# One comparison instead of four: the seat selection of an expert pair in a two-layer MoE kernel

## What is computed

```python
def hierarchical_moe(u, w_router_group, w_router_expert, w_gate, w_up, w_down):
    ...
    combine = (g_onehot[:, :, None] * (p_g[:, :, None] * w_in_group[:, None, :])).astype(x.dtype)
    y = jnp.zeros_like(x)
    for g in range(N_GROUPS):
        hid = jax.nn.silu(jnp.einsum('nd,edf->nef', x, w_gate[g])) * jnp.einsum('nd,edf->nef', x, w_up[g])
        y = y + jnp.einsum('nef,efd->nd', hid * combine[:, g, :, None], w_down[g])
```

## Time and profile before

| what | value |
|---|---|
| runs of the kernel before, median | 2497.47 us |
| profiled execution, its own time | 2503.42 us |
| profiled execution, span of the trace | 2501.6 us |
| TensorE matmul busy | 2353.1 us, 94% of the span |
| VectorE busy | 1884.0 us, 75% |
| ScalarE busy | 1359.9 us, 54% |
| HBM traffic | 241 GB/s over the span |

### The profile page before, as it was taken

How to read it: one execution, slowest core, us unless ns; L and a number is a source line. 1 busy time by engine, 2 the same in 40 slices (tenths; PEclk the granted TensorE clock), 3 DMA queues, 4 the chain that set the end, 5 groups by cost and what they waited for, 6 DMA issues and landing times.

```text
span 2501.6 us, 29914 instructions
## 1 busy us (share of the span) xinstructions
PE 2353.1 (94%) x11078; PEld 1732.6 (69%) x11078; DVE 1884.0 (75%) x2285; ACT 1359.9 (54%) x1497; POOL 20.5 (1%) x39
## 2 busy tenths in 40 slices
PE   7998999999997987999999998999989999988998
PEld 6556877777775465777777776456578865844987
DVE  2746999999997454999999998877467856564665
ACT  3235988898885142888888986126423312102332
POOL 0000000000000000000000000100000000000000
PEclk9998999999998988999999999999999999998999
DMA  9313988988886311788899888652156742532460
GB/s 330 114 68 146 375 355 365 379 358 354 354 366 255 134 68 67 322 362 357 357 370 380 359 358 334 208 184 103 68 195 242 278 151 101 200 136 76 165 240 18
DMA packets 115417, 603.67 MB, mean 241 GB/s; under 512 B 5208, under 2 KB 8352, under 8 KB 90556
## 3 DMA queue, kind: packets, MB, share of 16 engines
q1 hardware_dynamic: 111536, 588.83, 60.6%
q0 software_dynamic: 3792, 13.62, 1.6%
HBM read 601.38 MB, written 1.05 MB: 241 GB/s over the span
## 4 chain that ended last, share of the span: by engine, by line
PE 54%; DVE 20%; issue 13%; ACT 9%; DMA 2%; DVEq 1%; SPq 0%; ACTq 0%
PE bank L950 11%; DVE slab_parts L2640 8%; ACT high L1865 6%; PE bank L1260 4%; PE bank L1582 3%; PE bank L1212 3%; PE bank L1076 3%; PE bank L1239 3%; PE bank L1201 2%; PE bank L1511 2%; PE bank L1513 2%; PE bank L1512 2%; PE bank L1492 2%; PE bank L1494 2%; PE bank L994 2%
## 5 line engine op out<-in xcount | busy, mean ns | idle before, releaser
L2640 DVE TENSOR_TENSOR slab_parts<-ring,high 128x2048 fp32r<-128x2048 f32 x384 | 862.1, 2287 | 39.2 <-ACT high L1865 34.7
L1865 ACT ACTIVATE high<-ring 128x2048 fp32r<-128x2048 f32 x384 | 728.5, 1914 | 43.3 <-PE bank L1212 35.6
L1709 ACT ACTIVATE arena<-bank 128x512 f32<-128x512 f32 (+4 forms) x174 | 95.6, 587 | 401.5 <-PE bank L1582 90.3
L1212 PE MATMUL bank<-high,xT_parts 128*128 128x512 f32 x1024 | 294.3, 409 | 18.0 <-DVE slab_parts L2640 14.1
L1212 PE MATMUL bank<-slab_parts,xT_parts 128*128 128x512 f32 x1024 | 279.2, 394 | 0.0
L950 PE MATMUL bank<-ring,xT 128*128 128x512 f32 (+3 forms) x576 | 239.8, 578 | 9.1 <-ACT xT L1709 4.1
L1212 PEld LDWEIGHTS bank<-high,xT_parts 128*128 128x128 f32 x1024 | 184.5, 190 | 78.6 <-DVE slab_parts L2640 38.5
L1212 PEld LDWEIGHTS bank<-slab_parts,xT_parts 128*128 128x128 f32 x1024 | 194.0, 189 | 45.6
L1871 ACT ACTIVATE arena<-bank 64x512 f32<-64x512 f32 (+2 forms) x352 | 184.8, 534 | 62.4 <-PE bank L1239 52.1
L950 PEld LDWEIGHTS bank<-ring,xT 128*128 128x128 f32 x576 | 111.1, 194 | 135.4 <-issue 124.7
L2307 DVE TENSOR_TENSOR slab_parts<-ring,high 128x2048 fp32r<-128x2048 f32 x64 | 145.7, 2290 | 60.1 <-ACT high L1729 59.6
(11 more groups left out here) (373 smaller groups left out, 3536.1 us busy)
## 6 DMA issues: line engine op xcount, KB each, us to landing
ring<-in_moe_w_gate SPq DMA_DIRECT2D x64, 2048.0 KB, 8.6
ring<-in_moe_w_up SPq DMA_DIRECT2D x64, 2048.0 KB, 9.2
ring<-in_moe_w_down SPq DMA_DIRECT2D x64, 2048.0 KB, 9.0
ring<-in_mlp_w SPq DMA_DIRECT2D x32, 2048.0 KB, 12.8
ring<-in_w_mod SPq DMA_DIRECT2D x24, 2048.0 KB, 8.8
ring<-in_even_w_in SPq DMA_DIRECT2D x7, 2048.0 KB, 21.6
ring<-in_odd_w_in SPq DMA_DIRECT2D x6, 2048.0 KB, 10.5
ring<-in_h_w_in SPq DMA_DIRECT2D x6, 2048.0 KB, 8.1
```

Of the source, the lines that this page charges most:

```text
L1212: last = mm(dst[:, :], seated2[:, 4 * half + k, e], part_[:, k, :], start=(half == a == k == 0), stop=(half == a == 1 and k == 3))
L1865: act_fn(hi, weight_half(layer, name, half), ACT.Copy).then_inc(sem(f"high{layer}"), 1)
L2640: v.tensor_tensor(low, w, hi.bitcast(F32), ALU.subtract).then_inc(sem(f"low{layer}"), 1)
```

## The change

Each call of `take_seats` made four comparisons, one for each expert and tile, of the 64 seat numbers with one value per token (a scalar operand read per partition). It now makes one, of a tensor with a tensor: the seat numbers repeated over tiles and experts against the ranks repeated over the seats, 2 x 2 x 64 = 256 elements per partition. What is written to `sel` and the count on the semaphore stay the same.

```diff
             def moe_short(layer):
                 def take_seats(i):
 
-                    for e in range(2):
-                        for t in range(NT):
-                            last = v.tensor_scalar(sel[:, t, e], seats, rank[:, t, bass.ds(i * 2 + e, 1)], None,
-                                                   ALU.is_equal)
-                    last.then_inc(sem(f"seats{layer}"), 1)
+                    of_pair = [P, NT, 2, SEATS]
+                    v.tensor_tensor(sel, seats.unsqueeze(1).unsqueeze(1).to_broadcast(of_pair),
+                                    over(rank[:, :, bass.ds(i * 2, 2)], of_pair, 3), ALU.is_equal)\
+                        .then_inc(sem(f"seats{layer}"), 1)
```

## The result

| | before | after |
|---|---|---|
| median | 2499.80 us (6 runs, 2497.15 to 2503.64) | 2479.69 us (6 runs, 2476.49 to 2487.78) |
| span of the profiled execution | 2501.6 us | 2477.5 us |
| its mean granted clock | 0.964 | 0.971 |

The ratio is 0.9923, with an interval from 0.991 to 0.9936: faster by 0.77%, 20.1 us. Three more runs of the kernel before raised its median by 2.3 us over the 2497.47 that the forecast started from, so the gain was missed by 10.5 us and the time by 8.2.

What follows compares the result with a forecast made beforehand. TensorE was busy 94% of the span, but VectorE was taken to set the pace at the comparisons. 32 calls x 0.30 us = 9.6 us off the 2497.47 us median gave 2487.9 us, range 2485.0 to 2494.0.

Steps and rivals of the forecast that it cites:

- What a call gives back: On VectorE, four comparisons holding 0.65 us become one holding 0.35, so each call saves 0.30 us.
- How often, and that the round passes it on: 16 calls a layer count, 32 in all; each round of the expert layers shortens by the full 0.30 us.
- The clock in a round: Sign in the profile after: TensorE's granted clock in a round of the expert layers stays 1.00.
- the DMA share: The DMA engines' busy share of a first-layer round would go from 0.90 to 0.91.
- The idle time before `up1`: Sign on TensorE in a round: its idle time before `up1` falls from 0.46 to about 0.16 us.
- The 0.63 us of idle time: TensorE's whole idle time in a first-layer round, taken as room for the 0.30 us, leaving 0.33.
- Rival A: Gap where VectorE's first-layer loop turns: lost, gain 12.1 us (chance 0.09); also in the second layer, 7.1 us (0.08).
- the shift is only a dozen instructions: Argument against the loop-turn gap changing: VectorE's program moves by only a dozen instructions before each loop.
- the sum: Over both layers, 32 x 0.30 = 9.6 us, from the median of 2497.47 to 2487.9 us, 0.38% less.
- rival D: TensorE's low clock lasts longer at each layer's opening: 8 us more costs 8 us, giving 2495.9 us; chance 0.05.
- Rival E: VectorE instructions never overlap, so a call gives back 0.57 us: 18.1 us in all, 2479.4 us; chance 0.01.

Runs made afterwards that it cites:

- e8: The changed kernel with its one comparison issued twice, first into an unused buffer; 2495.45 us, ratio 0.9983 to the kernel before.
- e7: The changed kernel with six chained VectorE operations, 7.5 us, added at the end of the first layer's expert stage; 2491.33 us, ratio 0.9956 to the kernel before.
- e2: The changed kernel run again without any edit; 2479.88 us, ratio 0.9911 to the kernel before.
- e13: The kernel before, with four comparisons, delayed at the start by 2 memsets (1.9 us); 2501.57 us, ratio 1.0005 to the kernel before.
- e14: The changed kernel, with one comparison, delayed at the start by 2 memsets (1.9 us); 2485.15 us, ratio 0.9946 to the kernel before.
- e9: The kernel before, with dummy matmuls keeping TensorE busy in the mixer between the expert stages; 2499.09 us, ratio 1.0000 to the kernel before.
- e3: The kernel before, with four comparisons and 80 one-column memsets on VectorE at the start; 2495.62 us, ratio 0.9972 to the kernel before.
- e6: The kernel before with one comparison in the second layer only, four kept in the first; 2494.51 us, ratio 0.9970 to the kernel before.
- e17: The changed kernel with 90 one-column memsets on VectorE at the start; 2483.59 us, ratio 0.9927 to the kernel before.
- e4: The changed kernel with 24 one-column memsets on VectorE at the start; 2484.41 us, ratio 0.9932 to the kernel before.

## Why the prediction was wrong, and where it was right

**What a call gives back: right.** 0.30 was forecast, with 0.35 for the new instruction. It is 418 ns long and holds VectorE 0.33; the call gives back 0.32.

**How often, and that the round passes it on: right.** The second layer's rounds are 34.21 us (34.22 forecast), 0.32 less each; e8 shows the passing on by itself, 0.35 us for 0.34. Of the 32 calls of the 9.6 us, 30 lie in the rounds and openings of the table above, and they measured 4.49 + 4.49 + 2 x 0.32 = 9.6; the other two would make it 10.2. The clock in a round stayed 1.00, and the DMA share became 0.91 as worked out.

**The idle time before `up1`: wrong, without effect.** It should have fallen from 0.46 to 0.16 us. In the timeline of TensorE after, it is still 0.46:

```profile
516.51 1.09 PE L1212 MATMUL bank<-slab_parts,xT_parts 128*128 128x512 f32 x4
518.06 1.20 PE L1212 MATMUL bank<-high,xT_parts 128*128 128x512 f32 x4 [0.46 <-DVE slab_parts L2639]
```

I took the work ahead of `up1` as fixed. It moved as well: its last matmuls before the wait started 521.12 - 505.61 = 15.51 us after the `make_low` in front of the selection, and now 516.51 - 501.52 = 14.99. That is 0.52 less (0.32 of the call and 0.18 of the gap among it), and `up1` moved by the same. What shrank is TensorE's time counted as busy, from 34.10 to 33.66 us a round. The group of weight loads by form, before and after, shows where a part of it was: those of the `high` half of the down products waited 22.2 us in all for `make_low` before, and now 6.6.

```profile
L1239 PEld LDWEIGHTS bank<-high,hidden_parts 128*128 128x128 f32 x512 | 87.6, 190 | 43.0 <-DVE slab_parts L2640 22.2 <-DVE hidden_parts L2662 5.0 <-issue 4.2
L1239 PEld LDWEIGHTS bank<-high,hidden_parts 128*128 128x128 f32 x512 | 89.8, 190 | 28.1 <-DVE slab_parts L2639 6.6 <-DVE hidden_parts L2661 5.0 <-issue 2.2
```

In the second layer's round the same 171 matmuls at the same clock of 1.00 count 0.26 us less as busy (33.90 and 33.64), so some of the time counted as busy was waiting, for weights as it seems from these loads. The 0.63 us of idle time was not the reserve for which I took it; the reserve was larger.

**Rival A came true, with 0.09.** The first layer lost its gap and gave 2.8 us more, 12.4 in all (12.1 priced). Its price was right and the weight given to "the shift is only a dozen instructions" was not. The loop before reached past the border by at most 9 of its 64 instructions, so twelve instructions fewer ahead of it and six fewer in it were enough.

**The step that failed is the sum.** It ran "32 x 0.30 = 9.6 us" and let every stage outside the expert layers keep its time. With A it would have been 12.1, 2485.4 us, still inside the range. The remaining 7.7 us (20.1 - 12.4) lie in mid and in opening 2, where rival D looked, but D knew only a loss. In the two profiled executions this is time at the low clock, as the windows of the two pieces show: 8.1 and 5.2 us less lost to the clock, by the estimate there, for 7.9 and 4.7 us less time. Over all 20 profiles, opening 2 with one comparison ahead of it took 37.5 us on average, and in 6 of 12 it was 35.5 to 36.05 with a granted clock of 0.94 to 1.00 in its first 9.2 us; with four it took 39.6, and none of 8 had such a clock (0.57 to 0.67). In all 20 it is 34.7 to 35.7 us long without the time lost to the clock. Mid took 240.6 with one comparison in the first layer (11 profiles, e7 left out) and 243.5 with four (8). The tail is the same for both within 0.4 us, and the head scatters alike. That is some 5 us.

The unprofiled runs say the same in another way. Each carries its mean granted clock. Over 112 runs of the kernel before it is 0.9649, with a standard error of 0.0002; over the 11 of the kernel after (e2's among them) it is 0.9674, with 0.0007. A thousandth more goes with 1.2 us less in runs of one and the same kernel (278 runs, slope taken within kernels), and would be 2.5 us if TensorE's clock bounded the whole 2,480. So 0.0025 stands for 3 to 6 us of the 7.7. A higher granted clock between and at the opening of the rounds carries much of the rest of the gain; whether all, these numbers don't settle. The pair e13 and e14 has a rest of 5.8 us with the same mean clock, 0.9652, in both.

**What decides it stays open.** Not the arrival time alone (e8 arrives as late as before and keeps the clock), nor the chance of single executions (five pairs), nor attention alone (e9). A tendency with the arrival is there: in the nine profiles whose pair 16 of the first layer starts by 746.5 us mid is 240.1 us on average and never above 242.9, and e3 with its four comparisons is one of them (240.8); in the ten later ones it is 243.4, in seven of them above 243 (e7 left out). At opening 2 the low level comes at different times. In the profiles of before and after the fourteen filler matmuls that both kernels have ahead of the gathers (`keep_running`, L1138) take 1.81 us, and TensorE then waits 1.90 and 1.59 us for the first comparison's result. In e2, e6, e8 and e17 the same matmuls run at the low level, take 3.2 us and last until the gathers, and the opening itself has the high level, with 36.05 us. After first, then e2:

```profile
979.27 1.81 PE L1138 MATMUL bank<-resident 128*128 128x128 f32 x14
```

```profile
977.65 3.19 PE L1138 MATMUL bank<-resident 128*128 128x128 f32 x14
```

e8 is among these with two instructions that need as long as the four, so the length of the comparisons alone doesn't decide it either.

**Rival E gave 2479.4 us, nearly the time measured.** Its mechanism is refuted all the same: the new instruction is followed after 0.33 us, not 0.42, and the rounds gained 0.32 a call and not 0.57. A total that fits is no evidence for the way to it. The section of the Trainium skill that the prediction sets beside this rival ("VectorE: DVE Perf Modes", "The DRAIN you can't avoid") also says that a next instruction that is not held starts earlier; with that, the trace agrees: it starts 0.08 us before the end of the one in front.

## What to carry to other kernels

Where VectorE sets the pace of a loop, price an edit by the distance between starts (four comparisons of 248 ns hold 0.65 us, one of 418 holds 0.33), and multiply by the turns. A kernel whose TensorE clock falls between its full stages has a second account: savings of 10 to 12 us ahead of such stages brought 6 to 8 us more, and delays of 1.9 to 7.5 us cost 4 to 6 us more than themselves in the changed kernel, up to 2 in the kernel before, so the range must hold that on both sides. When two copies of one loop differ by a gap marked issue, look at where each stands in the engine's program and expect any edit ahead of it to move the gap.

## What the runs showed of the hardware that was not expected

- A loop on VectorE loses time on each turn when it stands across certain places of its program: 0.18 us a turn with the loop at 384 to 448, 0.10 with it further over the border (e13, e4), and more on the first turn (0.5 before). Eighty one-column writes far ahead of the loop made the kernel 0.28% faster ([0.9963, 0.9982]), their own time included.
- A wait of VectorE on its own result, counted against a register, held the next instruction up by 0.14 us (0.56 - 0.42) where the trace otherwise shows it 0.08 us ahead of the end of the one in front.
- A delay of 1.9 us at the start of the changed kernel cost 5.9 us of 2,480, one of 3.8 us cost 9.6, and one twice as long 11.1: small shifts were not additive.
- Filler matmuls in the mixer raised the granted clock in attention from 0.53 to 1.00 and changed the kernel before by 1.3 us (2500.37 to 2499.09), ratio 1.0000 [0.9989, 1.0012].
